# A two-layer trunk on one core: the first three units of a layer on tiles without the norm's root, the triangular inverse's end by halves, the final norm per token, and another order of the first loads

## The reference, cut to what matters

```python
def rms_norm(x, g, eps=1e-6):
    y = x * lax.rsqrt(jnp.mean(x * x, axis=-1, keepdims=True) + eps)
    return y * g
for l in range(2):
    h = rms_norm(x, mix_norm_g[l])
    p_gdn, p_mla, p_rwkv, p_dsa, p_gate = _split(h @ w_in[l], SLAB_SPLITS)
    ...                       # gated delta rule, latent attention, RWKV-7, sparse attention
    x = x + merged @ w_o[l]
    hm = rms_norm(x, mlp_norm_g[l])
    x = x + jnp.square(jax.nn.relu(hm @ w_up[l])) @ w_down[l]
return rms_norm(x, final_norm_g)
# rwkv7: p = p + (token_shift(p) - p) * mu, then low-rank products, decay, a recurrence
# both recurrences are computed in chunks of 64 tokens, with an inverse of (1 + lower triangle)
```

## Time and profile before

| | |
|---|---|
| median of 3 runs | 2073.06 us (2071.59 to 2074.18) |
| the profiled execution | 2073.46 us, span 2071.6 us, mean granted clock 0.991 |
| PE busy | 1995.8 us, 96% of the span, 13128 matmuls |
| DVE, ACT, POOL busy | 52%, 37%, 36% |
| chain that ended last | PE 87%, DVE 8%, ACT 3% |
| weights in flight | 268 transfers of 512 KB, 3.5 us each |

### The profile page before, as it was taken

How to read it: one execution, slowest core, us unless ns; L and a number is a source line. 1 busy time by engine, 2 the same in 40 slices (tenths; PEclk the granted TensorE clock), 3 DMA queues, 4 the chain that set the end, 5 groups by cost and what they waited for, 6 DMA issues and landing times.

```text
span 2071.6 us, 31700 instructions
## 1 busy us (share of the span) xinstructions
PE 1995.8 (96%) x13128; PEld 1535.3 (74%) x13128; DVE 1077.2 (52%) x1794; ACT 757.2 (37%) x1180; POOL 737.8 (36%) x550
## 2 busy tenths in 40 slices
PE   5999999999999999999989899999999999999997
PEld 4778787756667888888867777776566778888886
DVE  6685654896833422222367766369976343222223
ACT  4542513344353432322253353134344433322322
POOL 2540313322324444444435122143213344444442
PEclk8999999999999999999999999999999999999998
DMA  5320112221312333233332111123122222323231
GB/s 192 104 79 27 55 47 61 82 80 49 120 49 77 115 94 100 93 101 95 98 112 85 51 37 57 39 80 100 51 71 86 66 91 93 100 93 101 92 99 64
DMA packets 52254, 170.20 MB, mean 82 GB/s; under 512 B 5648, under 2 KB 13968, under 8 KB 51472
## 3 DMA queue, kind: packets, MB, share of 16 engines
q1 hardware_dynamic: 50928, 163.11, 24.6%
q0 software_dynamic: 1184, 5.07, 0.6%
HBM read 160.82 MB, written 7.34 MB: 81 GB/s over the span
## 4 chain that ended last, share of the span: by engine, by line
PE 87%; DVE 8%; ACT 3%; issue 1%; DMA 1%; SPq 0%; DVEq 0%; ACTq 0%
PE bank_a L476 14%; PE bank_a L477 13%; PE bank_a L482 13%; PE bank_v L482 7%; PE bank_v L476 7%; PE bank_v L477 7%; PE bank_v L542 4%; PE bank_v L620 3%; PE bank_a L762 1%; PE bank_f L574 1%; PE bank_f L580 1%; PE bank_f L553 1%; PE bank_a L751 1%; DVE arena L1444 1%; PE bank_f L575 1%
## 5 line engine op out<-in xcount | busy, mean ns | idle before, releaser
L437 POOL TENSOR_TENSOR w_lo<-ring,w_hi 128x512 fp32r<-128x512 f32 x536 | 731.4, 1385 | 1236.6 <-ACT w_hi L1132 1236.6
L476 PE MATMUL bank_a<-h_hi,w_hi 128*128 128x512 f32 x1312 | 530.8, 405 | 6.6 <-ACT w_hi L1132 6.6
L477 PE MATMUL bank_a<-h_lo,w_hi 128*128 128x512 f32 x1312 | 512.7, 391 | 0.0
L1132 ACT ACTIVATE w_hi<-ring 128x1024 fp32r<-128x1024 f32 x268 | 281.5, 1050 | 215.3 <-DVE arena L2012 212.4
L482 PE MATMUL bank_a<-h_hi,w_lo 128*128 128x512 f32 x1312 | 324.6, 389 | 0.0
L476 PEld LDWEIGHTS bank_a<-h_hi,w_hi 128*128 128x128 f32 x1312 | 247.2, 188 | 77.8 <-issue 19.4
L477 PEld LDWEIGHTS bank_a<-h_lo,w_hi 128*128 128x128 f32 x1312 | 247.3, 188 | 58.2 <-issue 8.1
L482 PEld LDWEIGHTS bank_a<-h_hi,w_lo 128*128 128x128 f32 x1312 | 246.0, 188 | 50.9
L476 PE MATMUL bank_v<-parts,w_hi 128*128 128x512 f32 x640 | 250.7, 392 | 1.4 <-DVE parts L1983 1.4
L477 PE MATMUL bank_v<-parts,w_hi 128*128 128x512 f32 x640 | 249.0, 389 | 0.0
L1444 DVE TENSOR_TENSOR sg<-bank_v,sg 128x512 f32<-128x512 f32 x112 | 77.5, 692 | 317.3 <-PE bank_v L482 245.8
(11 more groups left out here) (286 smaller groups left out, 2449.7 us busy)
## 6 DMA issues: line engine op xcount, KB each, us to landing
ring<-in_w SPq DMA_DIRECT2D x268, 512.0 KB, 3.5
out_ring<-in_w SPq DMA_DIRECT2D x64, 128.0 KB, 3.4
x_dram<-arena SPq DMA_DIRECT2D x2, 2048.0 KB, 9.6
arena<-x_dram SPq DMA_DIRECT2D x2, 2048.0 KB, 9.0
arena<-in_x SPq DMA_DIRECT2D x2, 1024.0 KB, 8.9
arena<-tabs POOLq DMA_DIRECT2D x4, 512.0 KB, 4.8
out_x<-arena SPq DMA_DIRECT2D x2, 1024.0 KB, 4.6
par<-in_par POOLq DMA_DIRECT2D x2, 937.0 KB, 7.4
```

Source lines behind the costliest of these rows:

```text
L437: ins = nc.gpsimd.tensor_tensor(w_lo[:, g % SPLIT, ks, :], raw, w_hi[:, g % SPLIT, ks, :].bitcast(F32), ALU.subtract)
L476: mm(b[:], w_hi[:, s, k, :], hi[:, k, :], start=k == 0, stop=False)
L477: mm(b[:], w_hi[:, s, k, :], lo[:, k, :], start=False, stop=False)
L1132: act_fn(w_hi[:, g % SPLIT, :, :], ring[:, g % RING, :, :], ACT.Copy).then_inc(S["split_hi"], 1)
```

## The change

Seven edits, in the order of the program.

1. SP loads the first constants (with the rotary frequencies), the positions, x, two units' weights, the other constants. POOL loads 82 columns of parameters and the rest after the second unit's weights. DVE makes the rotary arguments before it copies x; ACT the sines among the squares.
2. `RAW_UNITS` = 3: the first three units of a layer run on `x*gain`, without the root. ACT and DVE write these parts (`raw_hi`, `raw_low`), in layer 1 while the last down units run. The column sums stand before the last k of the first unit, the spread root in the second. DVE then scales the three banks with the root (`r_raw`) where ACT had copied them. The final h_hi and h_lo follow behind the third unit, k by k, and the fourth unit waits for them k by k.
3. In the rwkv inverse the block columns don't wait for ACT's copies, the spread rows stand after four of eight k of the gate, and ACT writes the block diagonal in eight operations.
4. The products with the values are made and negated ahead of the last x products.
5. `through` takes x by halves, u's first half first, in both inverses; `up` lies elsewhere.
6. At the end x times gain is transposed while the down units run; the root is applied to the token tiles, two on DVE and two on ACT.
7. Four stores of 128 tokens in place of two of 512 columns.

```diff
+RAW_UNITS = 3
...
-            sp.dma_start(consts[:, 0:2 * P], const_in[:, 0:2 * P]).then_inc(const_here, 16)
+            sp.dma_start(consts[:, 0:NFIRST], const_in[:, 0:NFIRST]).then_inc(const_here, 16)
+            sp.dma_start(POS["i"], pos_in.partition_broadcast(P)).then_inc(pos_here, 16)
             for half in range(2):
                 cols = slice(half * D // 2, (half + 1) * D // 2)
                 sp.dma_start(xin[:, :, cols], x_in.rearrange("(t p) d -> p t d", p=P)[:, :, cols]).then_inc(x_here[half], 16)
-            sp.dma_start(consts[:, 2 * P:], const_in[:, 2 * P:]).then_inc(more_here, 16)
-            sp.dma_start(POS["i"], pos_in.partition_broadcast(P)).then_inc(pos_here, 16)
...
+                if g == 1:
+                    sp.dma_start(consts[:, NFIRST:], const_in[:, NFIRST:]).then_inc(more_here, 16)
...
+            for i in range(2):
+                sp.wait_ge(S["o_out"], i + 1)
+                sp.dma_start(out[i * P:(i + 1) * P, :], xout[:, i, :]).then_inc(out_done, 16)
+                sp.wait_ge(o_out_act, i + 1)
+                sp.dma_start(out[(2 + i) * P:(3 + i) * P, :], xout[:, 2 + i, :]).then_inc(out_done, 16)
...
+            pool.dma_start(par[:, 0:NSMALL], par_in[0, :, 0:NSMALL]).then_inc(par_here, 16)
+            pool.wait_ge(w_here[1], 16)
+            pool.dma_start(par[:, NSMALL:], par_in[0, :, NSMALL:]).then_inc(par_rest, 16)
...
-                if between:
-                    between()
+                    if between and k + 1 == between[0]:
+                        between[1]()
...
+                    if last and before_last:
+                        before_last()
...
+                for half in range(2):
+                    pe.wait_ge(S[x + "_x"], at(l, x + "_x", 2 * (len(LEVELS) - 1) + half + 1))
+                    if x == "r":
+                        pe.wait_ge(S["r_y1"], at(l, "r_y1", half + 1))
+                    if half == 0:
+                        chunk_products("a", x + "_u", 0, V["x"], lambda m, p_: rhs[quarter(p_), m // H, quarter(m % H)])
+                        b0, reader, emptied = banks.next("a", x + "_wt")
+                        pe.wait_ge(reader, emptied)
+                        b1, reader, emptied = banks.next("a", x + "_wt")
+                        pe.wait_ge(reader, emptied)
+                    for f in range(2):
+                        for t in (2 * half, 2 * half + 1):
+                            k = f * TT + t
+                            for hp in range(2):
+                                h = 2 * f + hp
+                                last0 = mm(b0[quarter(hp), k * C:(k + 1) * C], V["e_tok"][0:C, t, quarter(h)], V["x"][0:C, t * H + h, :], start=True, stop=True)
+                                last1 = mm(b1[quarter(hp), k * C:(k + 1) * C], V["e_tok"][C:P, t, quarter(h)], V["x"][C:P, t * H + h, :], start=True, stop=True)
                 last0.then_inc(a_full, 1)
                 last1.then_inc(a_full, 1)
-                for half in range(2):
-                    chunk_products("a", x + "_u", half, V["x"], lambda m, p_: rhs[quarter(p_), m // H, quarter(m % H)])
+                chunk_products("a", x + "_u", 1, V["x"], lambda m, p_: rhs[quarter(p_), m // H, quarter(m % H)])
...
+            def by_tokens(m):
+
+                b, reader, emptied = banks.next("a", "o_tok")
+                pe.wait_ge(reader, emptied)
+                pe.wait_ge(S["n_g"], at(L, "n_g", m + 1))
+                for t in range(TT):
+                    ins = nc.tensor.transpose(b[:, t * P:(t + 1) * P], mg[:, m, t * P:(t + 1) * P], cst("ident"))
+                ins.then_inc(a_full, 1)
...
+                    for j in range(RAW_UNITS):
+                        if j == 1:
+                            root_spread = token_root(l)
                         g = begin_unit(("rw", next(rw)), l)
-                        b, reader, emptied = banks.next("a", "r_in")
+                        b, reader, emptied = banks.next("v", "r_raw")
                         pe.wait_ge(reader, emptied)
                         pe.wait_ge(S["split_lo"], g + 1)
-                        open_.append((g % SPLIT, b))
+                        s = g % SPLIT
                         for k in range(KT):
-                            pe.wait_ge(S["n_hi"], at(l, "n_hi", k + 1))
-                            mm(b[:], w_hi[:, g % SPLIT, k, :], h_hi[:, k, :], start=k == 0, stop=False)
-                            mm(b[:], w_lo[:, g % SPLIT, k, :], h_hi[:, k, :], start=False, stop=False)
-                    for s, b in open_:
-                        for k in range(KT):
-                            pe.wait_ge(S["n_h"], at(l, "n_h", k + 1))
-                            ins = mm(b[:], w_hi[:, s, k, :], h_lo[:, k, :], start=False, stop=k == KT - 1)
-                        ins.then_inc(a_full, 1)
+                            if j == 0 and k == KT - 1 and sums:
+                                sums()
+                            if j == 1 and k == 2:
+                                root_spread()
+                            if j == 0:
+                                pe.wait_ge(S["n_h"], at(l, "n_h", k + 1))
+                            mm(b[:], w_hi[:, s, k, :], h_hi[:, k, :], start=k == 0, stop=False)
+                            mm(b[:], w_hi[:, s, k, :], h_lo[:, k, :], start=False, stop=False)
+                            ins = mm(b[:], w_lo[:, s, k, :], h_hi[:, k, :], start=False, stop=k == KT - 1)
+                            if j == RAW_UNITS - 1 and k < KT - 1:
+                                ins.then_inc(S["n_raw"], 1)
+                        ins.then_inc(v_full, 1)
+                        raw_full[l, j] = banks.used["v"]
...
-                numbers = [gate(l, 2, 0, lambda: spread_rows(l, "r", R))]
+                numbers = [gate(l, 2, 0, (4, lambda: spread_rows(l, "r", R)))]
...
+                invert(l, "r", R, akk_values)
...
+            def spread_blocks(l, x, V):
+                act.wait_ge(S[x + "_sol"], at(l, x + "_sol", 1))
+                for j in range(C // BLOCK):
+                    cols = slice(j * BLOCK, (j + 1) * BLOCK)
+                    ins = act_fn(V["x"][:, :, cols], compact(V, 1), ACT.Copy, scale=cst("blocks_c")[:, j * BLOCK:j * BLOCK + 1])
+                ins.then_inc(S[x + "_x1"], 2)
...
+            def raw_hi(k):
+                act_fn(h_hi[:, k, :], xT[:, k, :], ACT.Copy, scale=pr("mix_g", k)).then_inc(S["n_hi"], 1)
+
+            def take_tokens(m):
+                act.wait_ge(a_full, filled.next())
+                b = filled.bank()
+                act_fn(xout[:, :, m * P:(m + 1) * P], b[:].rearrange("p (t n) -> p t n", n=P), ACT.Copy).then_inc(S["o_tok"], 1)
...
+                    for j in range(RAW_UNITS - 1):
+                        act.wait_ge(v_full, raw_full[l, j])
+                        split_next()
                     for k in range(KT):
+                        if k < KT - 1:
+                            act.wait_ge(S["n_raw"], at(l, "n_raw", k + 1))
+                        else:
+                            act.wait_ge(v_full, raw_full[l, RAW_UNITS - 1])
+                            split_next()
...
+                act_fn(POS["sin"][:, half, :], POS["red"][:, half, :], ACT.Sin)
+                act_fn(POS["cos"][:, half, :], POS["red"][:, half, :], ACT.Sin, scale=0.5).then_inc(S["tab_sin"], 1)
...
+            act.wait_ge(par_here, 16)
+            for k in range(KT):
+                act.wait_ge(S["x_t"], k + 1)
+                raw_hi(k)
+                if k == 3:
+                    split_next()
...
+                                if l + 1 < L:
+                                    act.wait_ge(par_here, 16 * (l + 2))
+                                    raw_hi(m)
                             split_next()
+                            if q == QUARTERS and l + 1 == L and m:
+                                take_tokens(m - 1)
...
+                v.tensor_copy(inv_rms, spread[:]).then_inc(S["n_spread"], 1)
+                dve.wait_ge(S["n_spread"], reached("n_spread"))
+                v.memset(R["rw"][:, :, 0:1], 0.0).then_inc(S["r_zero"], 1)
+                dve.wait_ge(S["r_zero"], reached("r_zero"))
+                for i, (number, b) in enumerate(units):
+                    dve.wait_ge(v_full, number)
+                    v.tensor_tensor(R["rw"][:, i % 4, 1:T + 1], b[:], inv_rms, MUL).then_inc(S["r_raw"], 1)
...
+            def raw_low(l, k):
+
+                dve.wait_ge(S["n_hi"], at(l, "n_hi", k + 1))
+                v.scalar_tensor_tensor(h_lo[:, k, :], xT[:, k, :], pr("mix_g", k), h_hi[:, k, :].bitcast(F32), MUL, SUB).then_inc(S["n_h"], 1)
...
+            for k in range(KT + 1):
+                if k < KT:
+                    dve.wait_ge(v_full, filled.next())
+                    b = filled.bank()
+                    v.tensor_copy(xT[:, k, :], b[:]).then_inc(S["x_t"], 1)
+                    dve.wait_ge(S["x_t"], reached("x_t"))
+                if k:
+                    raw_low(0, k - 1)
...
```

(15 more changed lines are left out.)

307 lines of the change are left out of this document (150 added, 157 removed).

## The result

The changed kernel takes **2046.96 us** (median of 4 runs, 2045.38 to 2049.51) where the kernel before took 2072.9 us on the same chip. The ratio is 0.9878, 95% interval [0.9865, 0.9890]: faster by 1.2%. The forecast was 2043.5 us, range 2036 to 2053. Direction and main mechanisms held; 3.5 us of the gain were missing.

The account below looks back on a forecast made before the run. TensorE, busy for 96% of the span, bounds the kernel, so only its waits count. Terms -8.5 - 8.0 - 7.0 - 1.5 - 5.8 + 1.3 = -29.5 us took 2073.46 to 2044.0; predicted median 2043.5, range 2036 to 2053.

Parts of the forecast that it names:

- Start of layer 0: From the kernel's start to the fourth unit: rotary chain, copies of x and raw low parts set the path; -8.5 us.
- Between the layers: Raw units replace the wait for sums, root, gain and split; third unit of layer 1 -8.5 us, -8.0 taken.
- Its last part comes about 0.5 us late: Fourth unit after the layer change: it takes the final h per k, whose last part comes about 0.5 us late.
- that disturbance: Start of layer 0: GpSimd beside VectorE stretches an operation from 0.71 to 1.71 us; two allowed, +2.0 us.
- What may be lost in between: Between the marks: late token-shift mixes, low-rank products and sums; +1.3 us for two layers, bounds 0 and +8.
- The lag of VectorE: Token-shift mixes: VectorE 4 us later, TensorE 9 ahead, a 13 us lag absorbed by VectorE's waits before 105.84.
- rival 1: Both layers: lag not absorbed; low-rank products, sums of squares or features come late, 4 us each; 2051.5 us, chance 0.14.
- rwkv inverse: Earlier block columns, block diagonal on ScalarE (first update of t -1.7), reordered end (-1.8): 2 x -3.5 = -7.0 us.
- Gated inverse: Gated branch: only the halves of u and wt change, its scan begins 0.75 us earlier; 2 x -0.75 = -1.5 us.
- The end: After the last product: 28 of 32 transposes moved ahead, first store issued at 2058.5 instead of 2064.30; -5.8 us.
- rival 4: First five units of each layer: TensorE stays at 1.2 GHz, 48 us lost less 4; 2087 us, chance 0.03.
- Those named for wrong: Raw units: waits for w_lo over 2 us each or half clock; end: last store over 4 us behind the first.

Follow-up runs that it names:

- experiment 5: Changed kernel with the positions issued behind both halves of x in SyncE's queue, not ahead of them: 2051.37 us.
- experiment 6: Changed kernel with each of ScalarE's eight squares of x behind a raw high part, not all ahead of the first weight split: 2045.52 us.
- Experiment 4: Changed kernel, but in layer 1 TensorE forms the column sums first and begins the three raw units only when the root is there: 2052.22 us.
- Experiment 2: Changed kernel with the low parts of the final h used last in the fourth unit and the low-rank products behind the sixth unit: 2042.49 us.
- experiment 1: Changed kernel, but the fourth unit forms its products with the high parts of h first and the eight with the low parts last: 2055.82 us.
- experiment 7: Changed kernel, but in the rwkv inverse ScalarE copies t before the gate's table load, sigmoid and weight split: 2048.42 us.
- Experiment 10: Changed kernel, but TensorE waits for both masked halves of y before the last level's products for x, in both inverses: 2049.67 us.
- experiment 9: Changed kernel with the end of both inverses as before: no halves, negated products behind the inverse, both masked y awaited: 2055.39 us.
- experiment 11: Changed kernel with its end as before: root spread, gain and 32 transposes behind the last product, two stores: 2054.44 us.

## Why the prediction was right, and where its sizes were off

**Start of layer 0: -8.5 forecast, -8.7 seen.** The path was the right one, and experiment 5 shows that the chain lies on it. Its terms were off and cancelled in part, which is luck. The positions were there at 6.27 and not at 4.5, and the first high part at 20.1 (begun at 19.35) and not at 18.6. From there copies and low parts took 11.2 us and not 12.0, so the last low part stood at 31.3 and not at 30.6. The third unit ended at 44.0 where the sum had 43.6; the forecast had allowed 0.6 more than its sum. TensorE had the full clock 3 us after unit 0's beginning (28.16) and kept it in the two units behind, as forecast. I did not see that ScalarE's squares held the first high part for 2 us (experiment 6).

**Between the layers: -8.5 for the third unit, -8.4 seen.** The wait for w_lo is 1.17 us where 1.0 was forecast; the clock stayed. Experiment 4 shows about half of the gain by itself.

**"Its last part comes about 0.5 us late": this is the step that failed.** It was 2.2 us, and in layer 0 too, where the forecast had no such term. I priced the low parts of the final h as the kernel before makes them, undisturbed. Now the splits of the fourth and fifth unit's weights fall beside them on GpSimd: four of the eight parts take 1.3 to 1.8 us in place of 0.68. Experiment 2 takes the wait away, with the one behind it, and wins 2.5 us per layer. The forecast had named that disturbance for the raw low parts (+2.0) and not for the next eight. The Trainium skill ("SBUF — State Buffer", section Who interferes with whom) states the exclusion between such VectorE operations and GpSimd; the trace agrees, with 1.78 us for the longest. "What may be lost in between", +1.3 for both layers, came out as 2.7 + 3.8 = 6.5: 4.4 are the late low parts, about 1.1 a fall of the clock behind them in layer 1 (last section), and 1.0 stays in small pieces.

**The lag of VectorE.** The 10.67 us of idle time before its first bonus product in layer 0 (10.79 before) say that it was absorbed there, as forecast. But rival 1 was nearer than its 0.14 suggests: experiment 1 has exactly its picture, the low-rank products late. In the changed kernel only 0.4 us of it shows, because the late low parts hold TensorE back.

**rwkv inverse: -7.0 forecast, -5.2 seen** (2.0 and 3.2). The small operations came 2.0 us earlier, the eight block operations took 2.45 us (2.35 forecast), and the sigmoid followed its table load at once (145.71, 147.00). But the first update of t gained 1.15 us in place of 1.7. ScalarE's copies ended at 149.0 and 149.5, within 0.2 us of the forecast (154.85 and 155.4, less the 6.0 us of the shift); the first masking of y then began 1.3 us behind the first copy, where one product of 0.93 had been put. The end gained 0.8 in layer 0 and 2.0 in layer 1 of 1.8 forecast. In layer 0 TensorE pauses twice there, 0.2 and 0.3 us, with nothing waited for ("issue"), and what hangs on it comes 0.9 us late; the same place in layer 1 has none. Why is open. The Trainium skill ("ScalarE: Activation LUTs", section What ACT_TABLE_LOAD costs) would add a drain of about 1.4 us to each switch; experiment 7 has one more row against it: load at 148.85, next operation at 150.15.

**Gated inverse: -1.5 forecast, -3.8 seen** (1.9 and 1.9). Halves of u and wt were priced, the other edit was not: the last products for x no longer wait for both halves of y. Experiment 10 gives it 0.9 and 0.7 us; experiment 9 gives both together 1.9 and 1.6, which leaves 1.0 and 0.9 for the halves, priced at 0.75. In rwkv the products of akk and the values stand between, so the order of the waits is worth nothing there.

**The end: -5.8 forecast, -5.7 seen.** All its steps held within 0.7 us; the first store is issued 5.8 us behind the last product, where 5.3 was forecast, and the last one 1.7 us behind the first. Taken back (experiment 11) it costs 6.3 by the marks, 7.5 +- 4 by the medians.

**The clock (rival 4)** did not decide. In the raw units half clock is there for the first 3 us of unit 0 alone. It came once more, behind the waits in the fourth unit of layer 1, for 3.4 us. In the kernel before it lay in the first and third unit of layer 0 and in the first of layer 1.

**The signs.** Those named for right came: no wait of TensorE over 2 us between the fourth unit and the scans (the longest is 1.7), the fourth unit at 44.03, the third unit of layer 1 14.1 us after the end of the last down product, and the first store 9.2 us after the last product (5.8, and 3.4 of transposes ahead of it). Those named for wrong did not, but for the 3 us of half clock in unit 0.

So the sum of the forecast was wrong by 4.1 us on the profiled execution: 4.6 lost around the fourth units beyond what was allowed, 1.8 missing in rwkv, against 2.3 more in the gated branch; the rest are tenths. That the total came within 4 us of the forecast owes something to the gated branch, whose second half of the gain was not forecast.

## What to carry to other kernels

When a wait is removed, price what the *next* consumer needs on its new date, with the disturbance that the neighbours cause on that date: an operation's duration from the old timeline holds only with the old neighbours. Waits stand in rows one behind the other; the size of the first does not tell what its removal brings, and a square of two edits (each alone, both) tells it. And an engine that takes over work to relieve another (the blocks on ScalarE) does it at the place of its own queue: look at what it had done early until then, and put that behind.
